# Two DeepNorm layers on one core: the residual added where units leave PSUM, a layer norm in place, and the feed-forward in pairs of blocks

## The reference

```python
for l in range(DEPTH):                        # DEPTH = 2, DN_ALPHA = 4 ** 0.25
    m = split(silu(c) @ w_ada[l] + b_ada[l], 6)   # shift, scale, gate, shift, scale, gate; another set for context
    y = mixing_sublayer(modulate(x, m[0], m[1]), ...)      # ... concatenated heads @ w_out[l]
    x = layer_norm(DN_ALPHA * x + m[2] * y, ln_g[l, 0], ln_b[l, 0])
    f = swiglu(modulate(x, m[3], m[4]), w_ffn_in[l], w_ffn_out[l])   # (silu(gate) * up) @ w2
    x = layer_norm(DN_ALPHA * x + m[5] * f, ln_g[l, 1], ln_b[l, 1])

def modulate(x, shift, scale): return x * (1.0 + scale) + shift
def layer_norm(x, g, b):                      # NORM_EPS = 1e-6, float32
    xc = x - mean(x)
    return xc * rsqrt(mean(xc * xc) + NORM_EPS) * g + b
```

## Time and profile before

| | us |
|---|---|
| median of 3 runs | 4574.81 |
| profiled execution | 4582.9 |
| its span, first to last instruction | 4580.9 |
| output projection, layer 0 / layer 1 (start of its first load to start of the next stage) | 1212.0 to 1350.0 / 3528.7 to 3636.4 |
| norm 0 | 1350.0 to 1466.4 / 3636.4 to 3729.5 |
| feed-forward | 1466.4 to 2426.2 / 3729.5 to 4492.4 |
| norm 1 | 2426.2 to 2542.8 / 4492.4 to 4580.9 |

### The profile page before, as it was taken

How to read it: one execution, slowest core, us unless ns; L and a number is a source line. 1 busy time by engine, 2 the same in 40 slices (tenths; PEclk the granted TensorE clock), 3 DMA queues, 4 the chain that set the end, 5 groups by cost and what they waited for, 6 DMA issues and landing times. The chain is left out here.

```text
span 4580.9 us, 54441 instructions
## 1 busy us (share of the span) xinstructions
PE 3831.0 (84%) x22562; PEld 3033.0 (66%) x22562; DVE 2045.3 (45%) x2209; ACT 1070.6 (23%) x1421; POOL 389.0 (8%) x280
## 2 busy tenths in 40 slices
PE   4999568939785999999997799469677859999996
PEld 2887446438674888888885688345366747777774
DVE  3111657646424343443445111766566234444445
ACT  1000322426314111111114100323245131111113
POOL 2000003002005000000002200010021040000000
PEclk6999679968797999999997899679888979999998
DMA  5222440041223111101104232240232121111111
GB/s 187 80 85 67 170 139 18 12 109 23 87 77 125 40 30 41 41 27 41 41 18 153 86 93 72 100 146 1 67 68 73 57 74 42 47 49 41 55 32 74
DMA packets 339927, 319.25 MB, mean 70 GB/s; under 512 B 42718, under 2 KB 310602, under 8 KB 339786
## 3 DMA queue, kind: packets, MB, share of 16 engines
q1 hardware_dynamic: 297514, 265.07, 18.6%
q0 software_dynamic: 6912, 30.15, 2.1%
q10 hardware_dynamic: 35360, 22.02, 1.5%
HBM read 248.17 MB, written 71.99 MB: 70 GB/s over the span
## 5 line engine op out<-in xcount | busy, mean ns | idle before, releaser
L478 PE MATMUL psum<-h_hi,f_whi 128*128 128x512 f32 (+1 forms) x1760 | 485.9, 374 | 70.4 <-DVE f_wlo L932 70.4
L937 DVE TENSOR_TENSOR y<-y,psum 128x1280 f32<-128x1280 f32 (+1 forms) x352 | 477.0, 1355 | 108.1 <-PE psum L478 106.2
L478 PE MATMUL psum<-h_lo,f_whi 128*128 128x512 f32 (+1 forms) x1760 | 481.6, 371 | 0.0
L478 PE MATMUL psum<-h_hi,f_wlo 128*128 128x512 f32 (+1 forms) x1760 | 481.4, 371 | 0.0
L478 PE MATMUL psum<-h_hi,w_hi 128*128 128x512 f32 (+1 forms) x1392 | 367.9, 367 | 117.0 <-DVE w_lo L552 117.0
L478 PEld LDWEIGHTS psum<-h_hi,f_whi 128*128 128x128 f32 x1760 | 307.0, 189 | 135.3 <-DVE f_wlo L932 70.9
L932 DVE TENSOR_TENSOR f_wlo<-f_raw,f_whi 128x1024 fp32r<-128x1024 f32 x132 | 161.0, 1221 | 481.4 <-ACT f_whi L903 423.9
L478 PE MATMUL psum<-h_lo,w_hi 128*128 128x512 f32 (+1 forms) x1392 | 366.4, 366 | 0.0
L478 PE MATMUL psum<-h_hi,w_lo 128*128 128x512 f32 (+1 forms) x1392 | 365.7, 366 | 0.0
L903 ACT CAST f_whi<-f_raw 128x1024 fp32r<-128x1024 f32 x132 | 138.3, 1048 | 905.1 <-PE psum L478 882.1
L478 PEld LDWEIGHTS psum<-h_lo,f_whi 128*128 128x128 f32 x1760 | 308.5, 188 | 59.4
(11 more groups left out here) (265 smaller groups left out, 5611.3 us busy)
## 6 DMA issues: line engine op xcount, KB each, us to landing
f_raw<-in_w_ffn_in SPq DMA_DIRECT2D x88, 512.0 KB, 5.7
w_raw<-in_w_in SPq DMA_DIRECT2D x48, 512.0 KB, 4.9
ada_w<-in_w_ada SPq DMA_DIRECT2D x24, 1024.0 KB, 10.9
proj_cm<-lin_stage POOLq DMA_DIRECT2D x38, 640.0 KB, 4.1
f_raw<-in_w_ffn_out SPq DMA_DIRECT2D x44, 512.0 KB, 3.6
ln_x<-x_cm SPq DMA_DIRECT2D x18, 1024.0 KB, 7.6
att_raw<-proj_cm SPq DMA_DIRECT2D x48, 320.0 KB, 5.7
x_cm<-ln_x SPq DMA_DIRECT2D x14, 1024.0 KB, 4.4
```

Of the source, the lines that this page charges most:

```text
L478: ins = nc.tensor.matmul(out[:, t0:t0 + tn], w, h[:, t0:t0 + tn], start=start and n == 0, stop=stop and n == 2)
L937: nc.vector.tensor_tensor(y[:, o, 0:tokens], y[:, o, 0:tokens], sets(o), ALU.add).then_inc(s_acc.h, 1)
```

## The change

1. Gates (modulation vectors 2 and 5) are divided by alpha after they are computed, and eps by alpha squared; so x + (gate/alpha)·y takes the place of alpha·x + gate·y, and the norm gives the same.
2. `mix_out` takes the place of `linear` for the output projection. The mixed heads come through a ring of three buffers; TensorE starts on a block as soon as it is split; old x is loaded into y behind them; each unit is added to y as it leaves PSUM, times its gate.
3. `residual_norm` works in place in y: no load of x, no alpha. ScalarE takes the root with eps as its bias straight from PSUM. The modulated input is computed by ScalarE from the normalised values with combined coefficients (scale·g and scale·b + shift), its low part by VectorE; new x = g·u + b is written in place, half by ScalarE, half by VectorE. x is stored to DRAM only in norm 1 of layer 0. GpSimd has nothing to do. The modulation vectors come as 8 pieces of 256 columns (`ModulationRows`), turned once at the end.
4. `swiglu` adds to y, which holds x, with the gate (no zeroing). The down part runs once for two blocks: six products a unit, one addition. Order on TensorE for a pair: gate of the even block, down of the pair before, up of the even block, gate and up of the odd block.
5. `linear` loses its branches for y; it stays for the input projections.

Core of the diff:

```diff
+def mix_out(k, l, tokens, h_hi, h_lo, y):            # RING = 3; streams(tokens): latent, context
+    # SyncE: mixed(0), weight(0), mixed(1), mixed(2), weight(1), mixed(3..7), x in two halves, weight(2..7)
+                def mixed(j):
+                    if j >= RING:
+                        sp.wait_ge(s_ylo.h, s_ylo.at(j - RING + 1))
+                    sp.dma_start(yin[:, j % RING, 0:tokens], k.y_dram[:, j, 0:tokens]).then_inc(s_in[j % RING].h, 16)
+    # ScalarE, VectorE: casts and subtractions in the same order; then on VectorE
+                def add(u):
+                    dve.wait_ge(s_mm.h, s_mm.at(u + 1))
+                    for m, t0, t1 in streams(tokens):
+                        ins = nc.vector.scalar_tensor_tensor(out=y[:, u, t0:t1], in0=sets[u % 2][:, t0:t1], scalar=gate[:, u, m:m + 1],
+                                                             in1=y[:, u, t0:t1], op0=ALU.mult, op1=ALU.add)
+                dve.wait_ge(s_x.h, s_x.at(32))
+                for u in range(KB):
+                    add(u)
+                    if u + 2 < KB:
+                        weight(u + 2)
+    # TensorE
+                for u in range(KB):
+                    pe.wait_ge(s_lo.h, s_lo.at(u + 1))
+                    if u >= 2:
+                        pe.wait_ge(s_ev.h, s_ev.at(u - 1))
+                    for j in range(KB):
+                        if u == 0:
+                            pe.wait_ge(s_ylo.h, s_ylo.at(j + 1))
+                        ins = three_products(...)
...
 def residual_norm
-        mod = ModulationTiled(k, st, 6, 7, mod_ranges, W=P, ring=3)
+        mod = ModulationRows(k, st, 6, mod_ranges, 3)
+            # ScalarE
+                square(0)
+                for i in range(n_c + (2 if last else 1)):
+                    if i < n_c:
+                        root(i)
+                        mod_copy(2 * i)
+                    if 1 <= i <= n_c and last:
+                        act.wait_ge(s_u.h, s_u.at(i))
+                        new_x(i - 1, KB, s_x)
+                    elif 1 <= i:
+                        if not last:
+                            modulated(i - 1)
+                    if i + 1 < n_c:
+                        square(i + 1)
+                    if i < n_c:
+                        mod_copy(2 * i + 1)
+                    if i >= 1 and not last:
+                        upper(i - 1)
+                        new_x(i - 1, XA, s_xa)
+            # TensorE
+                mean(0)
+                mean(1)
+                variance(0)
+                for i in range(n_c + 1):
+                    if i + 2 < n_c:
+                        mean(i + 2)
+                    if 2 * i < n_m and i < n_c:
+                        mod.product(pe, 2 * i)
+                    if i + 1 < n_c:
+                        variance(i + 1)
+                    if 2 * i + 1 < n_m and i < n_c:
+                        mod.product(pe, 2 * i + 1)
+                    if last and i >= 1:
+                        turn(i - 1)
+            # VectorE, per i: centre(i + 1), unit(i) (reciprocal, scaling), new_x(i - 1), lower(i - 1)
...
 def swiglu
-            @block.gpsimd
-                    nc.gpsimd.memset(y[:, j, 0:tokens], 0.0).then_inc(k.sem("y_zero").h, 1)
+                # VectorE, even block of a pair: lo(0, j + 1), gather of the pair before, then hidden product, lo(1, j + 1), ...
-                def down(j, q, last=False):
+                def down(p, last=False):
+                    pe.wait_ge(s_lo[2].h, s_lo[2].at(2) + p * 2)
+                    pe.wait_ge(s_ulo.h, s_ulo.at(2) + p * 2)
                     for o in range(KB):
...
+                        for q in range(2):
+                            ins = three_products(nc, sets(o + 1), chunks, d_hi[:, q, cols], d_lo[:, q, cols], u_hi[:, q], u_lo[:, q], q == 0, q == 1)
                         ins.then_inc(s_out.h, 1)
+                def pair(p, first=False):
+                    up(0, p * 2)
+                    if not first:
+                        down(p - 1)
+                        pe.wait_ge(s_acc.h, s_acc.at(-1) + p * KB)
+                    up(1, p * 2)
+                    up(0, p * 2 + 1)
+                    up(1, p * 2 + 1)
```

More of the change, by code:

```diff
@@ L485, in each_unit, with linear @@
         body(u, u % 2, u // 2)
-def linear(k, src, units, tokens, h_hi, h_lo, y, split=False, widths=None):
+def linear(k, src, units, tokens, h_hi, h_lo, widths=None):
     nc = k.nc
@@ L531, in _ @@
             def _(act):
-                for j in range(KB if split else 0):
-                    act.wait_ge(s_in[j // 2].h, s_in[j // 2].at(32))
-                    nc.scalar.copy(h_hi[:, j, 0:tokens], y[:, j, 0:tokens]).then_inc(s_yhi.h, 1)
                 def hi(u, s, turn):
@@ L545, in _ @@
                 dve.sem_inc(s_ev.h, 2)
-                for j in range(KB if split else 0):
-                    dve.wait_ge(s_yhi.h, s_yhi.at(j + 1))
-                    nc.vector.tensor_tensor(h_lo[:, j, 0:tokens], y[:, j, 0:tokens], h_hi[:, j, 0:tokens].bitcast(F32), ALU.subtract).then_inc(s_ylo.h, 1)
                 def lo(u, s):
@@ L712, in upper @@
+                    ins.then_inc(s_h.h, 1)
                 def upper(c):
[L713 to L734 removed]
@@ new lines, in upper, with new_x, mod_copy @@
+                    nc.scalar.copy(chunk(h_hi, c), hm[:, c % 2]).then_inc(s_hi.h, 1)
+                def new_x(c, blocks, done):
+                    for j in range(blocks):
+                        x = y[:, j, c * T:(c + 1) * T]
+                        ins = nc.scalar.activation(x, x, ACT.Identity, bias=b_ln[:, j:j + 1], scale=g_ln[:, j:j + 1])
+                    ins.then_inc(done.h, 1)
+                def mod_copy(u):
+                    if u < n_m:
+                        mod.copy(act, u)
+                        if u + mod.RING < n_m:
+                            mod.load(act, u + mod.RING)
@@ new lines, in _ @@
+                square(0)
[16 more added lines that the diff above has]
+                        new_x(i - 1, XA, s_xa)
+                    if i >= 2 and last:
+                        rows_copy(act, nc.scalar.copy, i - 2, 0)
@@ L782, in variance @@
                     ins.then_inc(s_var.h, 1)
-                mean(0)
-                for c in range(n_c + 1):
-                    for u in range(len(mod.pieces)):
-                        if mod_step(u) == c:
-                            mod.product(pe, u)
-                            if u:
-                                mod.turn(pe, u - 1)
-                    if c < n_c:
-                        variance(c)
-                    if c + 1 < n_c:
-                        mean(c + 1)
-                    if last and c >= 1:
-                        turn(pe, c - 1)
@@ new lines, in _ @@
+                if not last:
+                    g2, b2 = (v.unsqueeze(2).to_broadcast([P, KB, 2]) for v in (g_ln, b_ln))
+                    nc.vector.tensor_tensor(co[:, 0], scale, g2, ALU.mult).then_inc(s_co.h, 1)
+                    nc.vector.tensor_tensor(co[:, 1], scale, b2, ALU.mult).then_inc(s_co.h, 1)
+                    dve.wait_ge(s_co.h, s_co.at(2))
+                    nc.vector.tensor_tensor(co[:, 1], co[:, 1], shift, ALU.add).then_inc(s_co.h, 1)
+                centre(0)
+                for i in range(n_c + (2 if last else 1)):
+                    if i + 1 < n_c:
+                        centre(i + 1)
+                    if i < n_c:
+                        unit(i)
+                    if i >= 1 and not last:
+                        new_x(i - 1)
+                        lower(i - 1)
+                    if i >= 2 and last:
+                        rows_copy(dve, nc.vector.tensor_copy, i - 2, 1)
@@ L849, in swiglu @@
+    if last:
+        s_x.done(n_c)
+        s_t.done(n_c * TILES)
+        for x in s_row:
+            x.done(n_c)
+        for x in s_st:
+            x.done(16 * n_c * TILES // 2)
+    else:
+        for x in (s_h, s_hi, s_lo, s_xa, s_xd):
+            x.done(n_c)
+    if store:
+        s_out.done(16 * n_c)
 def swiglu(k, l, tokens, h_hi, h_lo, y):
@@ L1008, in swiglu @@
+                pair(0, True)
+                pair(1)
+                with pe.Fori(2, HP) as p:
+                    pair(p)
+                down(HP - 1, last=True)
     for n in range(3):
+        for x in (s_hi, s_lo):
+            x[n].done(HB)
         s_w[n].done(16 * HB)
-        for x in (s_hi, s_lo, s_mm)[:3 if n < 2 else 2]:
-            x[n].done(HB)
-    for x in (s_silu, s_h, s_uhi, s_ulo):
+    for x in (s_silu, s_h, s_uhi, s_ulo, *s_mm):
         x.done(HB)
     for x in (s_acc, s_out):
-        x.done(HB * KB)
```

476 lines of the change are left out of this document (239 added, 237 removed).

## The result

The changed kernel takes 4438.86 us (median of 4 runs, 4434.96 to 4446.22) beside 4576.44 us for the kernel before on the same chip: ratio 0.9698, 95% interval 0.9681 to 0.9715, 3.0% faster. The forecast was 4456 with a range of 4424 to 4494.

The account below looks back on a forecast made before the run. TensorE was taken to bound the feed-forward, a chain between engines the norms. Output projections 21, norms 63, feed-forward 35.5, less 0.2, made 119 us off the profiled 4582.9: 4464, or 4456 us by the median; range 4424 to 4494.

Parts of the forecast that it names:

- rival "full clock": Norm stages: TensorE at full clock throughout gives 36 us more gain, 4420 us; chance 0.08.
- the start of the output projections: Output projection: sign that its matmuls start 8 to 9 us after the first load of heads.
- the variance of layer 0: Norm stages of layer 0: sign that the variance stays at 5 to 6 us.
- the pairs: Feed-forward: two blocks take 84.5 to 84.7 us in layer 0, 65.3 to 65.6 in layer 1, no TensorE idle behind additions.
- the two bounds: Norm stages: full clock throughout gives 36 us more gain, low clock throughout 64 us less.
- The edit that speaks against the change: Layer 0 norms: ScalarE's adaLN copies queued before modulation and square make a chunk's chain 18.4 us, against 16.8 before.
- 2.2 us a block: Output projection: ring of three delivers three blocks per 6.5 us, 2.2 each, against 1.76 us for a block's products.
- the ring stutters: Output projection: the ring stutters or x comes late, 21 us of gain don't come, 4477 us; chance 0.1.
- the prediction's third sign of being wrong: Output projection: the prediction is wrong if VectorE's wait for x is followed by one of TensorE.
- The 2 us kept back in each layer: Feed-forward: 2 us per layer taken off the forecast gain for starts of units and of the loop.
- The rival that stalls only move: Feed-forward: stalls move to late additions or the hidden product, 35.5 us of gain don't come, 4491 us; chance 0.1.
- the one of the weight queue: Feed-forward: late gate-weight loads delay all eight additions; 4595 us at 13.5 us landing; chance 0.03, similar losses included.

Follow-up runs that it names:

- late-mean experiment: Changed kernel with the first mean of each of the four norms waiting for an added 1 MB load of x: 4472.89 us, ratio 0.9770.
- filled waits: Changed kernel with 8 or 24 unread TensorE matmuls before the second through last variance of each norm but the last: 4430.29 us, ratio 0.9678.
- single blocks: Changed kernel with the feed-forward's down products and gated additions run after each block instead of each pair: 4490.67 us, ratio 0.9816.

## Why the prediction was right, and where its terms were off

The forecast time was 17 us too high and the measured one lies within its range. It does so with norms that gained 31 us more than forecast, nearly the 36 us that were the price of the rival "full clock" (chance 0.08); 8 us missing in the output projections and the spread of the runs brought the sum back. So the mechanism held in the main, and the closeness of the number is in part luck. Of the signs named ahead, the start of the output projections, the variance of layer 0 and the pairs came as said; the lengths of the norm stages didn't (98.7, 102.2, 58.5 and 60.6 us for 108, 112, 65 and 66).

**The norms: right chain, mis-sized clock.** My stage for layer 0 was 16.2 us to the end of the first variance, 13.2 to the second, three cycles of 18.4, a tail of 22.4 and 0.8 for the modulation vectors. Measured: 1341.09 to 1352.8 = 11.7, then 12.4, then three cycles of 17.5, and 22.2 for the rest. Half the miss is the first term. I had TensorE start its first mean at the lower clock (5.6 us for one, and 5.9 for the variance); it comes straight from the output projection's matmuls with 2.03 us of idle, and both ran at full clock: mean 3.6, variance 3.72. That is 4.5 us in each of the four norms, 18 of the 31 us missing. The late-mean experiment shows that the means' part of it depends on the idle time; the variance's part it doesn't, for behind the slower means the first variance still took 3.72. The failed term is thus the 5.9 us for a variance that stands right behind two means, as much as the 5.6 for the mean. The rest is the cycle: variances at 5.15 to 5.8 where I took 5.9, in layer 1 3.6 to 3.7 until the fourth. So of the two bounds the full-clock one held at the front of every norm, and in the norm stages of layer 1; the slow variance that I took in the cycle of layer 0 was right, and the filled waits confirm its cause.

On this the Trainium skill, TensorE: Matmul & The Clock Gate, section "Loop structure matters more than you think", says that long waits between bursts bring the slow clock back. The runs agree for waits of 3.4 us and more (variance 5.11 to 6.76 us in every case), and 2.5 us were enough too (5.31 to 5.41). Behind 0.55 to 1.06 us it took 3.72, unless a wait of 3.9 us lay one product further back (5.13 to 6.76).

**The edit that speaks against the change.** The prediction said that the two copies in front of modulation and square lengthen the cycle (18.4 against 16.8 us before; measured 17.5). Confirmed and under-told: moving two instructions gives 54 us. What it didn't have is the second path of the same length, through the odd copy, cast, half of new x and root. With them where the change put them, the norms of layer 0 gained 32 us only because everything else in these stages got shorter.

**Output projection: the ring was too optimistic.** The start was right (8.56 us after the first load). The failed term is "2.2 us a block": the last two blocks came 3.7 us apart, the last one was split 27.0 us after the first load instead of 22.8, and the stage gained 8.3 for 12.5, in layer 1 4.7 for 8.5. In it the landing was taken at 3.5 us; the median of the eight loads was 5.5 us in layer 0 and 4.4 in layer 1. A load waits for a low part three blocks back, so a longer landing is paid several times. That the loads of weights and of x beside them made it longer wasn't tested. Five buffers give back 3.2 and 2.6 us. The rival "the ring stutters" was thus true for 8 of its 21 us. x came about when expected, a few us before it was needed in layer 0. By its letter, the prediction's third sign of being wrong, a wait of VectorE for x followed by one of TensorE, appears in layer 1, with 0.61 us; the rows put it down to the weight loaded behind x, which the prediction didn't price.

**Feed-forward: right, and no need to keep anything back.** Pairs of 84.48 and 65.28 us (forecast 84.5 to 84.7 and 65.3 to 65.6), the waits at the end 5.6 and 4.8 (5.8 and 5.0). The front came as forecast too: the first product starts 6.3 us into the stage for 10.2 before, in layer 1 6.2 for 8.5. The 2 us kept back in each layer for starts of units weren't there; that is most of the difference, 41.3 for 35.5, and 1.8 us are left without a place. The rival that stalls only move is refuted by the rows, as is the one of the weight queue: no wait of TensorE for a weight shows in the pairs. The reason given for the stalls was too narrow: it set one unit's products against one addition, where the single blocks show that products, addition and two hops share two sets. The gated addition takes 1.28 and 0.47 us for its two parts, 1.68 for both, where 1.6 was taken.

**The sum.** 119.5 us were forecast between the profiled executions, unrounded, and 147.9 came: +31.3 in the norms, +5.8 in the feed-forward, -8.0 in the output projections, -2.0 in the input projection and mixing, which nothing in the change touches and which varies by 4 us over the kernels run (985.9 to 989.8, one at 992.3), 1.1 outside these stages, and the 0.2 taken off for memsets. A part of the difference is chance, since the two profiled executions lie on opposite sides of their medians: by the medians the forecast was 17 us too slow.

## What to carry to other kernels

Lay every in-order queue of a pipelined stage beside the dependency chain: an instruction that nobody waits for (here a copy of a side product) costs its producer's whole path when it stands in front of one on which the chain hangs; put it behind. Price a TensorE stage by the idle time ahead of each burst, not by one clock for the stage: straight behind dense matmuls it mostly started fast here, behind a wait of several us slow, and shortening the chain may give the clock back as well. When units leave PSUM through two sets, compare two units' products with the products, addition and hops of one: an addition shorter than its products can stall them. Then give it more products (here two blocks at a time) before making it do more.

## What the runs showed of the hardware that I had not expected

- Equal matmuls (a variance: 16 of 256 columns, float32), over the profiled executions of the changed kernel and of the ten experiments: 5.31 to 5.41 us behind 2.5 us of idle in all twelve cases; behind 2.84 or 2.85 us, in the same place of the same instructions, 3.72 in eight cases and 5.37 to 5.41 in twelve; 5.11 to 6.76 behind 3.4 us and more. Behind 0.55 to 1.06 us they took 3.72, but 5.13 to 6.76 in the eight cases with one product and a wait of 3.9 us in front. The idle time right before is not the whole story; what else decides stays open.
- Unread matmuls that filled a wait to within 1.1 us of its end cost the chain nothing, and the variance behind them took 3.72 us in all ten cases.
- A gated addition from PSUM (scalar_tensor_tensor, float32) took 1.28 us for 1024 columns and 0.47 for 256; beside it the plain addition of 1280 took 1.49 (before).
